# A hybrid decoder layer: the HGRN output multiplied from packed score blocks, and another order of the scan's queues

## The reference

```python
def step(state, inp):                      # HGRN2, per chunk
    qi, ki, vi, bi = inp
    diff = bi[..., :, None, :] - bi[..., None, :, :]
    decay = jnp.exp(jnp.where(causal, diff, -jnp.inf))
    scores = jnp.einsum("bhtd,bhsd,bhtsd->bhts", qi, ki, decay)
    o = (jnp.einsum("bhts,bhsv->bhtv", scores, vi)
         + jnp.einsum("bhtd,bhdv->bhtv", qi * jnp.exp(bi), state))
    b_last = bi[..., -1:, :]
    state = (jnp.exp(b_last[..., 0, :])[..., :, None] * state
             + jnp.einsum("bhsd,bhsv->bhdv", ki * jnp.exp(b_last - bi), vi))
    return state, o
```

## Time and profile before

| | us |
|---|---|
| median of 3 runs | 1441.62 |
| lowest, highest | 1437.52, 1441.77 |
| the profiled execution | 1439.57 |
| its span, first to last instruction | 1437.5 |

### The profile page before, as it was taken

One profiled execution on the slowest core, in us unless ns is written; L12 is line 12 of the kernel. 1 busy time (PEld: TensorE's weight loads), 2 busy tenths in 40 slices (PEclk: granted clock), 3 DMA queues, 4 the chain that ended last, 5 costly groups with the idle time before them and its releaser, 6 DMA issues.

```text
span 1437.5 us, 22414 instructions
## 1 busy us (share of the span) xinstructions
PE 1398.9 (97%) x8579; PEld 1166.2 (81%) x8579; DVE 999.3 (70%) x1508; ACT 696.5 (48%) x1344; POOL 199.0 (14%) x225
## 2 busy tenths in 40 slices
PE   9999999999988888999999999999999999999998
PEld 7877888888877777878888888888888888888886
DVE  7584545561136777367897999999999575577567
ACT  6443456411366776256674343334444444454455
POOL 4000001101036655010000000000000144400000
PEclk9999999999998999999999999999999999999999
DMA  9642334446523433544442334335326766424213
GB/s 260 81 73 30 45 88 123 156 104 106 150 82 104 123 105 95 181 141 154 147 135 87 109 103 165 100 116 176 118 74 240 251 191 197 140 89 132 88 59 147
DMA packets 157866, 181.96 MB, mean 127 GB/s; under 512 B 25849, under 2 KB 96703, under 8 KB 157760
## 3 DMA queue, kind: packets, MB, share of 16 engines
q1 hardware_dynamic: 157760, 180.53, 43.3%
HBM read 130.43 MB, written 49.28 MB: 125 GB/s over the span
## 4 chain that ended last, share of the span: by engine, by line
PE 88%; DVE 4%; ACT 2%; DMA 2%; issue 2%; SPq 2%; DVEq 0%; ACTq 0%
PE psum L2538 9%; PE psum L2539 9%; PE psum L2540 9%; PE psum L2477 5%; PE psum L2479 5%; PE psum L2478 5%; PE psum L678 4%; PE psum L680 4%; PE psum L679 4%; PE psum L2450 4%; PE psum L2451 4%; PE psum L2452 4%; PE psum L736 3%; PE psum L738 3%; PE psum L737 3%; PE psum L1398 2%
## 5 line engine op out<-in xcount | busy, mean ns | idle before, releaser
L166 DVE TENSOR_TENSOR w_wlo<-w_raw,w_whi 128x1024 fp32r<-128x1024 f32 x66 | 87.8, 1332 | 231.9 <-ACT w_whi L151 231.7
L151 ACT ACTIVATE w_whi<-w_raw 128x1024 fp32r<-128x1024 f32 x66 | 69.7, 1059 | 177.0 <-PE psum L2452 80.2
L3271 DVE TENSOR_TENSOR g_slot<-w_raw,g_slot 128x512 fp32r<-128x512 f32 x77 | 62.5, 812 | 65.3 <-ACT g_slot L2845 65.3
L678 PE MATMUL psum<-h_hi,w_whi 128*128 128x512 f32 x256 | 100.7, 393 | 0.0
L680 PE MATMUL psum<-h_hi,w_wlo 128*128 128x512 f32 x256 | 99.7, 390 | 0.0
L679 PE MATMUL psum<-h_lo,w_whi 128*128 128x512 f32 x256 | 99.7, 389 | 0.0
L2845 ACT ACTIVATE g_slot<-w_raw 128x512 fp32r<-128x512 f32 x77 | 48.7, 632 | 104.8 <-PE psum L2479 99.6
L2450 PE MATMUL psum<-w_whi,m_hi 128*128 128x512 f32 x224 | 88.2, 394 | 0.9 <-DVE w_wlo L166 0.9
L2451 PE MATMUL psum<-w_wlo,m_hi 128*128 128x512 f32 x224 | 87.3, 390 | 0.0
L2452 PE MATMUL psum<-w_whi,m_lo 128*128 128x512 f32 x224 | 87.2, 389 | 0.0
L3529 POOL TENSOR_TENSOR mixed_home<-mixed_home 128x512 f32<-128x512 f32 x11 | 14.7, 1344 | 507.7 <-DMA mixed_home<-in_w_down 506.4
(11 more groups left out here) (463 smaller groups left out, 3883.1 us busy)
## 6 DMA issues: line engine op xcount, KB each, us to landing
w_raw<-in_w_up SPq DMA_DIRECT2D x39, 512.0 KB, 3.9
w_raw<-in_w_in SPq DMA_DIRECT2D x36, 512.0 KB, 6.3
s_rows<-pair_work SPq DMA_DIRECT2D x11, 1024.0 KB, 4.2
w_raw<-s_rows SPq DMA_DIRECT2D x44, 256.0 KB, 2.7
g_rows<-pair_work SPq DMA_DIRECT2D x18, 512.0 KB, 2.6
w_raw<-g_rows SPq DMA_DIRECT2D x33, 256.0 KB, 3.1
w_raw<-in_w_out SPq DMA_DIRECT2D x16, 512.0 KB, 4.5
mixed_home<-in_w_down SPq DMA_DIRECT2D x32, 256.0 KB, 3.4
```

What stands on the lines that cost most here:

```text
L678: pe.matmul(out, wh[:, w], self.hi[:, kt, part], start=(kt == 0), stop=False)
```

## The change

The packed score blocks are multiplied as they lie. The transfers, the tile `h_scores` and its clearing go, and `h_near` has one buffer. The HGRN output is now, for every head: four products on 32x32 tiles (each near block by its 32 rows of values), the state product, two products for level 6, and one of 64x64 for level 7 from a new tile `h_far`. They add up in bank 5. PE waits for its own earlier group before it adds onto the same rows, and `hd` is put between the last two groups.

The whole product of chunk c - 1 moves to the head of round c, behind `score(c, 0)`, `score(c, 1)`, `y64(c)` and before `score(c, 2)`. The queues of PE, ACT, DVE and SP are put in another order, POOL's stays. `hd` moves from bank 3 to 1, the mix of the GDN half from bank 2 to 7, the bank of level 7. DVE's masks and copies now wait for the HGRN product of the chunk before, and the values of the next chunk are loaded behind `oh(c)`.

```diff
@@ banks
-    BANK_OF = {"ks": 2, "solve": 3, "gd": 3, "og": 4, "oh": 5, "hd": 3, "turn": 2, "mix_g": 2, "mix_h": 5,
+    BANK_OF = {"ks": 2, "solve": 3, "gd": 3, "og": 4, "oh": 5, "hd": 1, "turn": 2, "mix_g": 7, "mix_h": 5,
@@ sp
-            self.sp_unpack(sp, c)
-            if c + 1 < NT:
-                self.done(sp, ("hd", c))
+                self.sp_lt_x(sp, c + 2)
+                self.done(sp, ("oh", c))
                 self.load_rows(sp, "v", c + 1, 2 * DG, self.hv)
-                self.sp_lt_x(sp, c + 2)
@@ pe_hgrn
-        pe.wait_ge(s["unpacked"], (c + 1) * (P // SB) * 16)
-        self.banks.released(pe, ("score", c, LEVELS))
+        for n in (LEVELS - 1, LEVELS):
+            self.banks.released(pe, ("score", c, n))
+        self.banks.released(pe, ("near", c))
...
+        near, far = self.near_heads(), self.packed(self.far)
         for h in range(NH):
-            if c:
-                pe.matmul(hs(out, h), hs(self.hqd, h), hs(self.hstate, h), start=True, stop=False)
-            ins = pe.matmul(hs(out, h), hs(self.sc, h), hs(self.hv, h), start=(c == 0), stop=True)
-        self.multiplied.mark(ins, ("oh", c))
+            for b in range(P // SB):
+                rows = slice(b * SB, (b + 1) * SB)
+                ins = pe.matmul(hs(out, h)[rows, :], near[rows, h, 0:SB], hs(self.hv, h)[rows, :], start=(h == 0), stop=False,
+                                skip_group_check=True)
+        self.multiplied.mark(ins, ("oh", c, 0))
+        if c:
+            for h in range(NH):
+                pe.matmul(hs(out, h), hs(self.hqd, h), hs(self.hstate, h), start=False, stop=False, skip_group_check=True)
+        self.done(pe, ("oh", c, 0))
+        for h in range(NH):
+            for b in range(0, P // SB, 2):
+                keys, queries = slice(b * SB, (b + 1) * SB), slice((b + 1) * SB, (b + 2) * SB)
+                ins = pe.matmul(hs(out, h)[queries, :], near[keys, h, SB:2 * SB], hs(self.hv, h)[keys, :], start=False, stop=False,
+                                skip_group_check=True)
+        self.multiplied.mark(ins, ("oh", c, 1))
         if c < NT - 1:
             self.banks.released(pe, ("turn", c))
             self.pe_products(pe, ("hd", c), self.BANK_OF["hd"], lambda h: hs(self.hkd, h), lambda h: hs(self.hv, h))
+        self.done(pe, ("oh", c, 1))
+        for h in range(NH):
+            ins = pe.matmul(hs(out, h)[P // 2:P, :], far[0:P // 2, h, :], hs(self.hv, h)[0:P // 2, :], start=False,
+                            stop=(h == NH - 1), skip_group_check=True)
+        self.multiplied.mark(ins, ("oh", c))
@@ pe, round c
+            if c:
+                self.pe_hgrn(pe, c - 1)
             self.pe_score(pe, c, 2)
             if c:
                 self.pe_dt64(pe, c)
             self.pe_score(pe, c, 3)
+            if c:
+                self.pe_solve(pe, c)
             if more:
                 self.pe_turn(pe, c)
             self.pe_score(pe, c, 4)
-            if c:
-                self.pe_solve(pe, c)
             self.pe_score(pe, c, 5)
             if more:
                 self.pe_y32(pe, c + 1)
+            self.pe_outputs(pe, c)
             if c:
                 self.pe_mix(pe, c - 1, 0, self.BANK_OF["mix_h"])
             self.pe_score(pe, c, 6)
-            self.pe_outputs(pe, c)
-            self.pe_score(pe, c, 7)
             if c:
                 self.pe_mix(pe, c - 1, 1, self.BANK_OF["mix_g"])
             if more:
                 self.pe_dt32(pe, c + 1)
                 self.pe_dx(pe, c + 1)
-            self.pe_hgrn(pe, c)
+            self.pe_score(pe, c, 7)
+            if more:
+                self.pe_ks(pe, c + 1)
             self.pe_score(pe, c + 1, 0)
             self.pe_score(pe, c + 1, 1)
             if more:
                 self.pe_y64(pe, c + 1)
-                self.pe_ks(pe, c + 1)
+        self.pe_hgrn(pe, NT - 1)
@@ act, round c
             if c:
                 self.act_inverse(act, c, 1)
-            if c:
+                self.act_exp(act, c, 3)
                 self.act_exp(act, c, 4)
+                self.act_squares(act, c - 1, 0)
                 self.act_root(act, c - 1)
-                self.act_exp(act, c, 5)
+                self.act_vn(act, c)
             if more:
                 self.act_keys(act, c)
+            if c:
+                self.act_exp(act, c, 5)
             self.act_exp(act, c, 6)
-            if c:
-                self.act_vn(act, c)
...
-            self.act_squares(act, c, 1)
             if c:
                 self.act_mix(act, c - 1, 1)
+            self.act_squares(act, c, 1)
             self.act_exp(act, c + 1, 2)
             self.act_key_decay(act, c + 1)
-            self.act_exp(act, c + 1, 3)
-            self.act_squares(act, c, 0)
+        self.act_squares(act, NT - 1, 0)
@@ dve_near, dve_place
-        if c >= 2:
-            dve.wait_ge(self.s["unpacked"], (c - 1) * (P // SB) * 16)
+        if c:
+            self.done(dve, ("oh", c - 1))
...
+        here = self.packed(self.far)[0:ahead] if n == LEVELS else self.near_heads()[0:P - ahead, :, SB:2 * SB]
+        ins = dve.tensor_copy(here, data)
@@ dve, round c
             if c:
-                self.dve_dx(dve, c)
                 self.dve_differ(dve, c, 3)
+                self.dve_rhs(dve, c)
+                self.dve_differ(dve, c, 4)
+                self.dve_dt(dve, c, 1)
+                self.dve_differ(dve, c, 5)
+                self.dve_hstate(dve, c - 1)
+                self.dve_outputs(dve, c - 1)
...
-            if c:
-                self.dve_hstate(dve, c - 1)
-                self.dve_differ(dve, c, 4)
-                self.dve_rhs(dve, c)
-                self.dve_differ(dve, c, 5)
-                self.dve_dt(dve, c, 1)
-                self.dve_outputs(dve, c - 1)
             self.dve_near(dve, c)
             self.dve_differ(dve, c + 1, 1)
             self.dve_place(dve, c, 6)
+            if more:
+                self.dve_state(dve, c)
+            self.dve_query(dve, c)
             if c:
                 self.dve_mix(dve, c - 1, 0)
             else:
                 self.slabs.remainder(dve, self.front.first["q"] + NH + 1)
-            if more:
-                self.dve_state(dve, c)
-            self.dve_query(dve, c)
-            self.dve_place(dve, c, 7)
-            self.dve_differ(dve, c + 1, 2)
             self.dve_dt(dve, c + 1, 0)
+            self.dve_dx(dve, c + 1)
             if c:
                 self.dve_mix(dve, c - 1, 1)
+            self.dve_differ(dve, c + 1, 2)
+            self.dve_place(dve, c, 7)
```

More of the change, by code:

```diff
@@ L1275, in __init__ @@
             self.ed, self.ql, self.kl = k.ed, k.ql, k.kl
-            self.sc, self.hqd, self.hkdt, self.hkd, self.hstate, self.hv = (
-                t("h_" + n) for n in ("scores", "qd", "kdt", "kd", "state", "v"))
+            self.sc_gap, self.hqd, self.hkdt, self.hkd, self.hstate, self.hv = (
+                t("h_" + n) for n in ("gap", "qd", "kdt", "kd", "state", "v"))
             self.gate = [t("h_gate"), t("g_gate")]
             self.on = t("normed", DM)
-            self.near = [t(f"h_near{i}", DG // 2) for i in range(2)]
+            self.near, self.far = t("h_near", DG // 2), t("h_far", DG // 2)
             self.middle = t("h_middle", NT * NH)
@@ L1286, in __init__ @@
                  "expd", "levels", "q_decay", "k_decay", "queried", "keys", "squared", "rooted", "inverted", "mixed_hi", "elast",
-                 "placed", "unpacked", "middles")
+                 "placed", "middles")
         self.s = {n: k.sem("s_" + n) for n in names}
@@ L1307, in near_part, with near_heads @@
         return ap[:, at:at + NH * width].rearrange("p (h t) -> p h t", h=NH)
-    def near_heads(self, c):
-        return self.near[c % 2][:].rearrange("p (h t) -> p h t", h=NH)
+    def near_heads(self):
+        return self.near[:].rearrange("p (h t) -> p h t", h=NH)
     def packed_blocks(self, ap, m):
@@ L1349, in load_rows @@
         sp.dma_start(tile[:], self.front.rows_out[c * P:(c + 1) * P, at:at + DG]).then_inc(self.s[name + "_in"], 16)
-    def sp_unpack(self, sp, c):
-        self.banks.released(sp, ("score", c, LEVELS - 1))
-        self.banks.released(sp, ("near", c))
-        if c:
[L1356 to L1360, removed]
     def sp(self, sp):
@@ L1777, in dve_near @@
         self.done(dve, ("score", c, self.NEAR))
-        if c >= 2:
-            dve.wait_ge(self.s["unpacked"], (c - 1) * (P // SB) * 16)
-        bank, blocks = self.banks.of(("near", c)), self.near_heads(c)[:, :, 0:SB]
+        if c:
+            self.done(dve, ("oh", c - 1))
+        bank, blocks = self.banks.of(("near", c)), self.near_heads()[:, :, 0:SB]
         for n in range(self.NEAR + 1):
@@ L1800, in dve_place @@
         data = self.packed(self.banks.of(key))[0:P - ahead, :, 0:ahead]
-        if n == LEVELS:
-            if c:
-                self.done(dve, ("oh", c - 1))
-            ins = dve.tensor_copy(heads(self.sc[:])[0:ahead, :, ahead:P], data)
-        else:
```

(10 more changed lines are left out.)

## The result

The changed kernel takes 1462.3 us in the median (1459.74 to 1466.24, four executions), against 1441.69 us before (1437.52 to 1442.44, four). The ratio is 1.015, with an interval of 1.012 to 1.018: 20.6 us slower. The forecast was 1447, with a range that ends at 1462, just short of it. The direction was right; of the size the forecast had a quarter, 5 us above the median before where 20.6 came.

A forecast was written before the change was run, and what follows sets the result against it. PE bounds the scan, held once per chunk by the score transfers. Saving 3.9 us per chunk but adding PE work and 3.6 of waits gives 20.8 us chunks, +7 us on 1439.57: 1447 us, range 1430 to 1462.

The forecast's parts named there:

- The gaps are 1.5 us at most, so I leave the clock at full: PE's new waits in each chunk: taken as too short to lower TensorE's clock, so no slow-clock time was added.
- rival (b): Low clock returns in some chunks of the scan: 1.7 us per chunk, 12 us more, 1459 us; chance 0.12.
- round: One inner chunk of the scan on PE: 20.8 us, of which 17.2 work and 3.6 waits.
- PE's own work: PE per chunk at full clock: 15.3 us before; 17.2 after, as 14.6 plus 19 shape changes at 0.135.
- the waits: PE's three new round trips to other engines in each chunk, together 3.6 us.
- The near blocks: 32 HGRN output products on 32x32 tiles: different tiles run at once, 8 rounds, 0.86 us.
- rival (c): Row tiles on one PSUM bank run one after another: 3.5 us per chunk, 28 more, 1475 us; chance 0.08.
- Wait (1): PE's GDN output waits for its bank, which DVE frees last in its series with the normed outputs: 0.7 us.
- Wait (2): PE's `dt32` waits for the bank that ACT frees in the inverse: 1.2 us.
- wait (3): PE's score 7, sharing a bank with the GDN mix, waits for DVE's mix remainder: 1.5 us.
- The ends: First product 0.8 us later, first round 0.9 longer, last chunk 21.2 us against 20.5.
- The removal: Transfers' stall, 2.4 us per chunk, and the slow clock behind it, 1.5, go: together 3.9 us per chunk.

The follow-up runs named there:

- run 1: Changed kernel plus idle matmuls, 4 ahead of `dt32` and 7 ahead of score 7, in each chunk but the first and last: 1456.1 us.
- run 5: As run 1, plus idle matmuls in the last chunk: 8 ahead of the outputs, 7 ahead of score 7, 3 ahead of the last product: 1449.0 us.
- run 8: Changed kernel with DVE's remainder of the GDN mix put ahead of its two copies for `dt32` and `dx`: 1456.8 us.
- run 2: Kernel before, plus 11 idle matmuls per chunk where PE waits for the unpacked scores: 1430.67 us.
- Run 4: Order alone: the changed kernel's queues and banks with the old kernel's product form, tiles and four transfers: 1446.3 us.
- run 10: As run 9, plus idle calls in the first chunk, 2 ahead of score 4 and 11 ahead of `y32`: 1437.3 us.
- run 3: Form alone: the old kernel's queues and banks with the changed kernel's product, tiles and DVE masks, no transfers: 1433.7 us.
- run 9: As run 3, plus two idle calls ahead of the outputs in every chunk, and 3 and 2 in the last chunk: 1433.8 us.
- run 11: As run 10, plus 9 more idle calls in the first chunk, ahead of the HGRN product: 1430.58 us.

## Why the prediction was right in direction and short in size

**The step that failed** is "The gaps are 1.5 us at most, so I leave the clock at full". After has half clock behind its waits of 1.05 and 1.7 to 1.8 us, some 1.1 us apart, in every inner round (granted clock 0.86 to 0.94); with both filled it is 1.00 there (runs 1 and 5), and the kernel takes 1449.0 us instead of 1462.3. So rival (b) is what happened, and it had a chance of 0.12. Its price was nearly right: 12 us, where run 5 against after is 13.3 by the medians and 1.9 in each inner round. The other 2 us of the miss are run 5's 1449.0 against the forecast's 1447.

The argument against (b), that the rounds with the low clock had a gap of 2 to 3 us before them, took the shortest gap seen to matter as the shortest that matters. The trace of before had more to say, and not all on one side:

```profile
420.28 1.13 PE L1398 MATMUL psum<-s_g_rn,rows_stage 128*128 128x128 f32 x8 [1.33 <-ACT hgrn_q L894]
...
475.74 0.46 PE L1542 MATMUL psum<-s_h_state,s_h_qd 128*128 128x128 f32 x2 [2.17 <-DMA s_h_scores<-s_h_near]
```

Behind a wait of 1.33 us eight 128x128 instructions take 1.13, full clock. And the one chunk of the earlier trace rows at 1.00 starts behind a wait of 2.17 us, as long as that ahead of the chunk from 455.87, which had 0.91. So the length of a wait alone did not tell the clock behind it, and the term should have been bounded from both sides, by zero and by the 1.7 us, with the forecast somewhere between.

**What held**, by the timeline of run 5 at full clock (the last stretch is 2.95 to the near blocks, from 516.95 to 519.90, and 5.19 for the HGRN block, from 498.88 to 504.07):

| step | forecast | measured |
|---|---|---|
| end of the far half to the GDN output | 6.0 | 5.54 |
| from there to `dt32` | 4.51 | 4.50 |
| `dt32` and `dx` | 0.95 | 1.04 |
| to score 7 | 1.66 | 1.80 |
| score 7 to the end of the far half | 7.7 | 8.14 |
| round | 20.8 | 21.02 |

The sum of the round is right in part by luck, as two errors cancel. PE's own work was put at 17.2 us and is 18.0 (its busy time in run 8 at a clock of 1.00); the waits were put at 3.6 (the three named make 3.4) and come to 3.0. The low count shows in the old kernel too. The prediction gives it 15.3 us, where its own row of the chunk at 1.00 has PE busy for 15.81, and closes the sum with 1.5 us for the clock, where the same rows give 19.78 - 18.68 = 1.1. In the table the missing work is mostly the last stretch, 8.14 for 7.7.

**The near blocks**, named as the likeliest to fail, held. The row of the line itself, in after's chunk from 460.93 (duration in ns, smallest, median and largest; first and last start; form):

```profile
L1532 PE MATMUL psum<-s_h_v,s_h_near x32: 267/268/292, 460.9 to 461.7; 32*32 32x128 f32 x32
```

All 32 start within 0.8 us, and the next group starts 1.00 after the first: that is the 0.86 of work and 0.14 for the change of shape of the forecast. One after another they would have taken 3.46. So rival (c) fell. Its source, the rule of the Trainium skill, "TensorEngine Tiling (Array Packing)", Restrictions and Gotchas, that row tiles cannot access the same PSUM bank simultaneously, is not what these rows show, and the measurement decides. The estimate by the 3.07x of "TensorE: Matmul & The Clock Gate", Part 3, 1.13 us plus the change, is also above the row.

**Wait (1)**, forecast at 0.7, is about 0.2 (in run 5 `gd` starts at 508.44 and the output at 509.61, 1.17 for 1.0 of work). **Wait (2)** was 1.05 for 1.2, **wait (3)** 1.7 to 1.8 for 1.5. DVE's timeline in after's chunk from 484.03 shows the first and the third:

```profile
490.99 0.68 DVE L1781 TENSOR_TENSOR s_h_ed<-hgrn_f 128x512 f32<-128x512 f32 x1
491.60 1.11 DVE L1853 SCALAR_TENSOR_TENSOR s_h_state<-s_h_state,s_h_elast,psum 128x128 f32<-128x128 f32 x4
492.63 0.15 DVE L1865 TENSOR_TENSOR s_stat<-s_stat,gdn_small 128x4 f32<-128x4 f32 x1
492.81 1.13 DVE L1873 SCALAR_TENSOR_TENSOR s_normed<-psum,s_stat,s_h_gate 128x128 f32<-128x128 f32 x4
...
500.85 0.43 DVE L1759 COPY_PREDICATED rows_stage<-mask,psum 96x256 f32<-96x256 uint32 x1
501.31 0.28 DVE L1769 COPY rows_stage<-psum 32x128 f32<-32x128 f32 x1
501.63 0.75 DVE L1882 SCALAR_TENSOR_TENSOR m_lo<-psum,cols,m_hi 128x512 fp32r<-128x512 f32 x1
```

From start to start the difference takes 0.61 and the statistic 0.18, where the forecast had 0.75 and 0.39 (the earlier trace rows have 0.72 and 0.39). These are 0.35 of the 0.5 us by which the output comes sooner than forecast. The small instruction lasts 0.36 there and 0.15 here; what made it longer before was not looked into. Behind `dx` the two copies take 0.46 and 0.32 where the forecast had 0.36 and 0.24, and from the mix remainder to score 7 it is 0.90 for 0.82: that is the larger third wait.

**The ends.** From the scan's first product behind the wait for `hgrn_q` (420.28 before, 419.52 after) to the first HGRN output product it is 0.6 us less, and not 0.8 more. That is chance: PE waits 1.65 us for `lt_rows` in after's profiled execution and 2.30 in before's, and 3.11 in run 1's. The first round was forecast 0.9 longer, 20.0; run 5 has 20.1, after has 25.51 by its clock of 0.73. The last chunk, product to projection, was forecast at 21.2; run 5 has 21.6, after 23.4.

**The removal** was right: no row of transfers is left, and run 2 shows the clock's part of it, 0.9 to 1.6 us per chunk for the 1.5. Run 4 shows what the sum had not asked: the order alone already hides the transfers, so in the new order the form removes nothing and adds some 2 us.

## What to carry to other kernels

A wait that a change puts on TensorE is to be priced with the clock behind it, also where it is only 1 to 2 us long, as here; where it can't be taken away, idle matmuls in it are cheap, and in this kernel they gave the best version of either form. When a change contains two cures of one stall, try each alone: the stall is saved once, both prices are paid. Where PE waits for an engine in the middle of its own series, walk that engine's queue from start to start: here it gave the three waits to within 0.5 us. And when a sum is checked against the old kernel, check its terms one by one against a row at full clock, for two wrong terms can close it.

## What the runs showed of the hardware that was not expected

- Waits of 1.05 and 1.7 to 1.8 us within one round bring TensorE to half clock (0.86 to 0.94 over the five inner rounds, after). Four and seven idle calls in them keep it at 1.00 (runs 1 and 5). The length of a wait does not decide it alone: 2.17 us stand ahead of a chunk at 1.00 and of one at 0.91 (before), and behind 0.74 us the clock was 0.50 for some 10 us in after and 1.00 in run 5.
- The low clock does not end when PE is busy again. In run 1 the clock was 0.50 over 7.77 us with PE busy for 7.68. In run 10 the mean was 0.58 over 27.7 us with PE busy for 27.47: at half clock for (1 - 0.58) x 2 x 27.7 = 23 us. Elsewhere it is over within a round. What sets its length stays open; no run was made to tell it.
- Executions of one program fall into two groups 7 us apart (runs 3 and 9, 1430 and 1437) with mean granted clocks of 0.997 and about 0.991. Filling the first chunk's waits up to the product (run 11) brought the spread down to 0.9 us.
- Four row tiles of 32x32 write one bank side by side: 32 instructions with 128 moving columns in 1.00 us.
